# The causal mask of forgetting attention: from a bf16 product to an addition to the row of gate sums, row tiles in reverse order

## The reference

```python
log_f = jax.nn.log_sigmoid(f_logit.astype(jnp.float32) + f_bias.astype(jnp.float32))
cum = jnp.cumsum(log_f, axis=1)
...
s = jnp.einsum('bqhd,bkhd->bhqk', qb, k, preferred_element_type=jnp.float32) * scale
s = s + cb[..., None] - cum_k[:, :, None, :]
...
s = jnp.where((k_pos[None, :] <= q_pos[:, None])[None, None], s, NEG_INF)
p = jax.nn.softmax(s, axis=-1)
return jnp.einsum('bhqk,bkhd->bqhd', p.astype(v.dtype), v)
```

## Time and profile before

| What | Value |
|---|---|
| median of 3 runs | 2323.47 us |
| lowest and highest | 2323.45 and 2328.69 us |
| time of the profiled execution | 2331.4 us |
| its span, first to last instruction | 2329.6 us |
| TensorE matmul busy (PE) | 2255.2 us, 97% of the span |
| TensorE weight loads (PEld) | 1839.1 us, 79% |
| VectorE (DVE) | 1198.5 us, 51% |
| ScalarE (ACT) | 854.2 us, 37% |
| GpSimd (POOL) | 567.6 us, 24% |
| mean granted TensorE clock | 0.988 |
| the bf16 mask products, L1825, 128 of them | 29.4 us busy, 230 ns each |

### The profile page before, as it was taken

How to read it: one execution, slowest core, us unless ns; L and a number is a source line. 1 busy time by engine, 2 the same in 40 slices (tenths; PEclk the granted TensorE clock), 3 DMA queues, 4 the chain that set the end, 5 groups by cost and what they waited for, 6 DMA issues and landing times.

```text
span 2329.6 us, 32539 instructions
## 1 busy us (share of the span) xinstructions
PE 2255.2 (97%) x11512; PEld 1839.1 (79%) x11512; DVE 1198.5 (51%) x1885; ACT 854.2 (37%) x1526; POOL 567.6 (24%) x423
## 2 busy tenths in 40 slices
PE   7998898999999999999999999999899999999998
PEld 6876686888888788877888777778688888878887
DVE  5659568444444434337332476646844444443432
ACT  3127334333333312222221477733433333331223
POOL 2423332222232000110000366643222222200011
PEclk9999998999999999999999999999999999999999
DMA  7340441322221613223442877544122222162312
GB/s 230 98 105 2 154 154 33 96 87 82 81 81 63 246 56 131 90 74 117 145 153 99 219 178 179 138 153 146 37 90 87 87 88 81 63 230 72 131 48 79
DMA packets 253241, 261.20 MB, mean 112 GB/s; under 512 B 15968, under 2 KB 221024, under 8 KB 248176
## 3 DMA queue, kind: packets, MB, share of 16 engines
q1 hardware_dynamic: 242160, 220.32, 31.8%
q10 hardware_dynamic: 11008, 39.92, 4.4%
HBM read 187.92 MB, written 65.08 MB: 109 GB/s over the span
## 4 chain that ended last, share of the span: by engine, by line
PE 89%; DVE 6%; DMA 2%; ACT 1%; POOL 1%; issue 1%; SPq 0%; ACTq 0%; DVEq 0%
PE psum L1713 12%; PE psum L1714 12%; PE psum L1715 12%; PE psum L1983 11%; PE psum L1985 11%; PE psum L1987 11%; PE psum L1861 3%; PE psum L1886 3%; PE psum L1961 2%; PE psum L1963 2%; PE psum L1962 2%; PE psum L1821 1%; PE psum L1822 1%; DVE b_full L1453 1%; DVE set_lo L1472 1%; DVE b_lo L1438 1%
## 5 line engine op out<-in xcount | busy, mean ns | idle before, releaser
L1983 PE MATMUL psum<-b_hi,a_hi 128*128 128x512 f32 x1232 | 484.6, 393 | 20.6 <-DVE b_lo L1438 20.6
L1987 PE MATMUL psum<-b_hi,a_lo 128*128 128x512 f32 x1232 | 482.7, 392 | 0.0
L1985 PE MATMUL psum<-b_lo,a_hi 128*128 128x512 f32 x1232 | 482.6, 392 | 0.0
L1983 PEld LDWEIGHTS psum<-b_hi,a_hi 128*128 128x128 f32 x1232 | 233.4, 189 | 72.5 <-issue 24.1
L1713 PE MATMUL psum<-set_hi,dw_hi 128*128 128x512 f32 x704 | 274.8, 390 | 3.2 <-DVE set_lo L1472 3.2
L1714 PE MATMUL psum<-set_lo,dw_hi 128*128 128x512 f32 x704 | 273.9, 389 | 0.0
L1715 PE MATMUL psum<-set_hi,dw_lo 128*128 128x512 f32 x704 | 273.9, 389 | 0.0
L1985 PEld LDWEIGHTS psum<-b_lo,a_hi 128*128 128x128 f32 x1232 | 233.5, 190 | 48.6 <-issue 0.5
L1987 PEld LDWEIGHTS psum<-b_hi,a_lo 128*128 128x128 f32 x1232 | 233.3, 189 | 49.0
L782 POOL TENSOR_TENSOR a_sum<-a_raw 128x512 f32<-128x512 f32 x88 | 114.6, 1302 | 501.2 <-DVE a_lo L1433 442.7
L748 POOL TENSOR_TENSOR score<-score,inv_l 128x128 f32<-128x128 f32 (+7 forms) x128 | 144.9, 1147 | 355.6 <-DVE inv_l L1319 353.9
(11 more groups left out here) (205 smaller groups left out, 3604.0 us busy)
## 6 DMA issues: line engine op xcount, KB each, us to landing
a_raw<-in_ffn_w_gate_up SPq DMA_DIRECT2D x88, 512.0 KB, 5.1
hid_scr<-hid_out SPq DMA_DIRECT2D x44, 512.0 KB, 5.7
set_full<-hid_scr SPq DMA_DIRECT2D x22, 1024.0 KB, 6.2
x_t<-x_scr SPq DMA_DIRECT2D x16, 1024.0 KB, 8.3
dw_raw<-in_ffn_w_down SPq DMA_DIRECT2D x32, 512.0 KB, 3.8
x_scr<-x_t ACTq DMA_DIRECT2D x24, 512.0 KB, 2.6
w_raw<-in_fox_w_in SPq DMA_DIRECT2D x22, 512.0 KB, 4.0
w_raw<-in_swa_w_out SPq DMA_DIRECT2D x16, 512.0 KB, 4.1
```

What stands on the lines that cost most here:

```text
L1983: T.matmul(out_ps, a_hi[i][:, j, :], b_hi[i][:, j, :], start=not more and j == 0, stop=False, skip_group_check=True)
L1985: T.matmul(out_ps, a_hi[i][:, j, :], b_lo[i][:, j, :], start=False, stop=False, skip_group_check=True)
L1987: last = T.matmul(out_ps, a_lo[i][:, j, :], b_hi[i][:, j, :], start=False, stop=j == KH - 1, skip_group_check=True)
```

## The change

The list of steps is turned round: (7), (6), (5), (4), (2, 3), (0, 1). `group` now counts the tile pairs in the order in which they come, and `place` says where a result belongs; the buffers of `fox_p` swap addresses with it. The matmul L1825 is gone. Instead VectorE adds `causal_bf` to the 128 columns of `cum_all` that lie on the tile's diagonal, in place, ahead of the tile's pass. As the tiles come from last to first, a column that has been masked is no longer read by the later ones, which are narrower. The pass waits for the addition by a semaphore, `cum_turn`; in a double step the second addition also waits for the first pass. The residual `x_t` is now loaded with two of its parts after the last PV but one.

```diff
-        fox_p = [[at(f"fox_p{e}{g}", (6 * e, 12 + 8 * e)[g], [P, (6, TT)[g], 2 * P]) for g in range(2)] for e in range(2)]
+        fox_p = [[at(f"fox_p{e}{g}", (16 + 6 * e, 8 * e)[g], [P, (6, TT)[g], 2 * P]) for g in range(2)] for e in range(2)]
...
-                self.tiles = [(0, 1), (2, 3), (4,), (5,), (6,), (7,)] if self.fox else [(t,) for t in range(TT)]
+                self.tiles = [(7,), (6,), (5,), (4,), (2, 3), (0, 1)] if self.fox else [(t,) for t in range(TT)]
...
-                self.blocks = [[[(0, 0, 1), (1, 0, 2)]], [[(2, 0, 3)], [(3, 0, 4)]]] + \
-                    [[[(t, 0, 4)], [(t, 4, t - 3)]] for t in range(4, TT)] if self.fox else [[0]] * TT
+                self.blocks = [[[(t, 0, 4)], [(t, 4, t - 3)]] for t in range(TT - 1, 3, -1)] + \
+                    [[[(2, 0, 3)], [(3, 0, 4)]], [[(0, 0, 1), (1, 0, 2)]]] if self.fox else [[0]] * TT
...
+            def turns_of(self, s):
+
+                return 2 * len(self.tiles[s]) - 1
+
+            def cum_turn(self, u, e, s):
+
+                turns = [self.turns_of(i) for i in range(self.steps)]
+                return 2 * sum(turns) * u + 2 * sum(turns[:s]) + e * turns[s]
+
...
-                    if a.fox and t0 == 2:
+                    if a.fox and t0 == 4:
                         sp.wait_ge(a.pv_done, a.total)
...
-                dve.wait_ge(a.qk_done, n + 1)
                 if a.fox:
                     if s == 0:
 
                         dve.wait_ge(cum_in[e], 16 * u + 16)
-                    apart(dve)
-                    for i, t in enumerate(a.tiles[s]):
+                    else:
+
+                        wait(dve, a.max_done, n - 1)
+                    cum, turn = fox_cum(u, e), a.cum_turn(u, e, s)
+                    for i, t in reversed(list(enumerate(a.tiles[s]))):
                         here = slice(fox_at(t), fox_at(t) + fox_w(t))
-                        last = V.tensor_tensor_reduce(out=score[sl][:, here], in0=ps[:, here],
-                                                      in1=fox_cum(u, e)[:, 0:fox_w(t)],
+                        V.tensor_tensor(cols(cum, t * P), cols(cum, t * P), causal_bf[:, :], ALU.add).then_inc(cum_turn, 1)
+                        dve.wait_ge(a.qk_done, n + 1)
+                        dve.wait_ge(cum_turn, turn + a.turns_of(s) - 2 * i)
+                        apart(dve)
+                        last = V.tensor_tensor_reduce(out=score[sl][:, here], in0=ps[:, here], in1=cum[:, 0:fox_w(t)],
                                                       scale=SCALE, scalar=3.0e38, op0=ALU.add, op1=ALU.min,
                                                       accum_out=neg_max[sl][:, i:i + 1])
+                        if i:
+                            last.then_inc(cum_turn, 1)
+
+                            dve.wait_ge(cum_turn, turn + a.turns_of(s) - 1)
                     last.then_inc(a.max_done, 1)
                     return
...
-                            diagonal = cc + ww == w
                             T.matmul(ps, q_hi[:, qs], key[:, cc:cc + ww], start=True, stop=False)
-                            last = T.matmul(ps, q_lo[:, qs], key[:, cc:cc + ww], start=False,
-                                            stop=not diagonal)
-                            if diagonal:
-                                last = T.matmul(ps[:, ww - P:ww], ident_bf[:, :], causal_bf[:, :], start=False,
-                                                stop=True)
+                            last = T.matmul(ps, q_lo[:, qs], key[:, cc:cc + ww], start=False, stop=True)
```

More of the change, by code:

```diff
@@ L397, in group, with place @@
             def group(self, s):
+                return self.groups - 1 - self.place(s) if self.fox else s
+            def place(self, s):
                 return self.tiles[s][-1] // 2 if self.fox else s
+            def turns_of(self, s):
[3 more added lines that the diff above has]
+                return 2 * sum(turns) * u + 2 * sum(turns[:s]) + e * turns[s]
             def completes(self, s):
-                return not self.fox or self.tiles[s][-1] % 2 == 1
+                return not self.fox or self.tiles[s][0] % 2 == 0
         SWA_EARLY = 2
@@ L410, in trunk @@
         swa_row = sem("swa_row")
+        cum_turn = sem("fox_cum_turn")
         keys_in = [sem(f"keys_in{i}") for i in range(2)]
@@ L453, in fox_copied @@
             if f > fox.local(e, s):
-                return fox.p_dve, 2 * (fox.steps - 1) * u + 2 * (s - 1) + e + 1
+                return fox.p_dve, 2 * (fox.steps - 1) * u + 2 * s + e + 1
             return fox.p_act, 2 * fox.steps * u + 2 * s + e + 1
@@ L932, in probs_high @@
                 g = a.group(s)
-                par = g % 2
+                par = a.place(s) % 2
                 if not a.fox and s % 2:
@@ L952, in result_high @@
                 if a.fox:
+                    k = a.place(s)
                     apart(act)
-                    nc.scalar.activation(o_hi[g // 2][:, bass.ds(u, 1), g % 2 * 2 * P:(g % 2 + 1) * 2 * P],
+                    nc.scalar.activation(o_hi[k // 2][:, bass.ds(u, 1), k % 2 * 2 * P:(k % 2 + 1) * 2 * P],
                                          bank[O_BANK][:, 0:2 * P].unsqueeze(1), ACT.Copy).then_inc(a.oh_done, 1)
@@ L1330, in probs_copy @@
                 g = a.group(s)
-                if a.fox and s:
+                if a.fox and a.fills[s] > 1:
                     wait(dve, a.pv_done, a.groups * u + g - 1)
                     dve.wait_ge(a.t_done, a.fill(u, e, s) + 2)
-                    for dst, src in fox_pieces(a.blocks[s][1], a.bank_of(e, s, 1)[0], fox_p[e][g % 2]):
+                    for dst, src in fox_pieces(a.blocks[s][1], a.bank_of(e, s, 1)[0], fox_p[e][a.place(s) % 2]):
                         last = V.tensor_copy(dst, src)
@@ L1345, in result_low @@
                 if a.fox:
-                    at0 = (slice(None), bass.ds(u, 1), slice(g % 2 * 2 * P, (g % 2 + 1) * 2 * P))
-                    V.tensor_tensor(o_lo[g // 2][at0], bank[O_BANK][:, 0:2 * P].unsqueeze(1), o_hi[g // 2][at0].bitcast(FP32),
+                    k = a.place(s)
+                    at0 = (slice(None), bass.ds(u, 1), slice(k % 2 * 2 * P, (k % 2 + 1) * 2 * P))
+                    V.tensor_tensor(o_lo[k // 2][at0], bank[O_BANK][:, 0:2 * P].unsqueeze(1), o_hi[k // 2][at0].bitcast(FP32),
                                     ALU.subtract).then_inc(a.o_free, 1)
@@ L1866, in pv @@
                 g = a.group(s)
-                par, t = g % 2, a.tiles[s][-1]
+                par, t = a.place(s) % 2, 2 * a.place(s) + 1
                 pb = bank[O_BANK]
@@ L1877, in pv @@
                     pe.wait_ge(v_crossed[u // 2], 32)
-                if g == 0 and a.fox:
+                if s == 1 and a.fox:
                     pe.wait_ge(a.v_in[b], 8 * (u - b + 2))
```

1 line of the change is left out of this document (added).

## The result

The changed kernel takes 2397.0 us (median of four runs, 2391.24 to 2400.43); the kernel before, run beside it, took 2326.08 (2323.45 to 2331.74). The ratio is 1.0299, 95% interval 1.0267 to 1.0331: 3% slower. The side was forecast, the size was not: 2332.0 with a range up to 2347.

A forecast was written before the change was run, and what follows sets the result against it. TensorE's stream was taken as the bound. Stage work 220.8 us plus 22.5 idle gave 243.3 against 232.3 (+11.0), the end -2.4, together +8.6: 2332.0 us on the median, range about 2319 to 2347.

The forecast's parts named there:

- Part 1: TensorE's saturated stream: dropping 128 mask products of 0.0625 us saves 8.0 us; bounds 5 and 20.
- Part 2: VectorE: 128 additions hold it 0.32 us each (bounds 0.2, 0.45), 5.1 us a pair, raising 18.8 to 23.9.
- The self-wait: VectorE, pass waiting for its own addition's semaphore: adds 0.03 us to the addition's 0.29.
- this sum: Whole kernel: stage +11.0 us and end -2.4, together +8.6 us.
- Part 3: Reversed order: TensorE waits 1.85 us for step 8's norm in each of 8 pairs, 14.8; bounds 1.2 and 2.3.
- Part 4: Reload of the gate sums delays TensorE another 0.5 us in 7 pairs, 3.5 us; bounds 0 and 1.0 each.
- Part 5: Stage's start and end: 4.2 us TensorE idle at the start; earlier x_t load gives -2.4 at the end.
- The clock rival: TensorE's granted clock falls after repeated waits, 1.7 us each, eight of them 14: 2346 us; chance 0.08.
- The other slow rival, the reload: VectorE's run from reload to tile 5's norm stretches, 1.3 us a pair, 9 in all: 2341 us; chance 0.16.
- The first: Fast rival: additions and order are hidden, TensorE loses nothing after the fill: 2315 us; chance 0.13.
- The second: Fast rival, half the stall: TensorE waits 0.9 us a pair, no second wait: 2321 us; chance 0.18.

The follow-up runs named there:

- the kernel without a mask: Kernel before without the bf16 mask product and nothing in its place: 2323.40 us against 2330.69, ratio 0.9970.
- The PSUM variant: Changed kernel with the mask added to the scores in PSUM instead of to the gate sums in SBUF: 2350.37 us, ratio 1.0086 to the kernel before.
- order-only kernel: Changed kernel with its reversed order, but the mask product back on TensorE and no VectorE additions: 2335.4 us, ratio 1.0023 to the kernel before.
- The kernel with two SBUF operands in before's order: Kernel before, mask product kept, plus 128 unused VectorE additions of 128 columns, both operands in SBUF: 2393.36 us, ratio 1.0267.
- the variants without the contention: Changed kernel with mask added in PSUM (2350.37 us), GpSimd's norm cut to 128 columns (2340.32), or most additions issued before the reciprocal (2352.84).

## Why the prediction was right on the side and wrong on the size

**Part 1 held.** 8.0 us forecast, 7.0 measured in the kernel without a mask.

**Part 2 is the step that failed.** It priced an addition at 0.32 us with a bound of 0.45, by the slope of wider passes. Those passes have one operand in PSUM; none of the rows it went by was an SBUF-to-SBUF operation beside a norm, and it never asked which engine runs beside the addition. This is its group between 1350 and 1550 (busy us, mean ns, idle before):

```profile
L1312 DVE TENSOR_TENSOR cum_all<-cum_all,causal_bf 128x128 f32<-128x128 f32 x91 | 76.0, 835 | 4.5 <-DMA cum_all<-cum_scr 3.7
```

At 0.83 us in the mean, and with the 0.15 from its end to the start of the pass (1422.86 to 1423.01), it is 16 x (0.83 + 0.15 - 0.32) = 10.6 us a pair more than costed. A pair came out 7.3 longer than the forecast 28.3 (35.6 in the mean), so at least 3 us of that were slack. That GpSimd starts later because VectorE is held closes the ring: VectorE waits out GpSimd's instruction, GpSimd waits for VectorE's reciprocal, and VectorE shows 86% busy, GpSimd 50%.

A smaller error lies in the same step. The self-wait was priced at 0.03 us, by the chain in the earlier trace rows. In the rows above, an addition of 0.28 lets the pass start 0.43 us after its own start when the pass waits for its semaphore (1401.84 to 1402.27), and 0.20 after it when the next operation doesn't (1411.87 to 1412.07). The difference is 0.23 us, though the second of the two rows is a reciprocal and not a pass. Of a chain of copies the Trainium skill ("VectorE: DVE Perf Modes", section "The DRAIN you can't avoid") states that a semaphore after each cost nothing extra. These rows disagree where the next operation waits for that semaphore.

The contention isn't all that was missing. The PSUM variant's additions take 0.29 us, and it still costs 20 us where this sum had 8.6. How that rest divides wasn't measured.

**Part 3 held in place; its size was nearer to the low bound.** The stall was forecast at 1.85 us with the additions and 1.2 without them. The order alone shows 1.0 to 1.1. With additions of 0.29 us in PSUM it is 1.33. In the changed kernel the wait at that place is 1.38, and eight more of 0.18 to 1.17 us stand in the same pair, which the prediction didn't have.

**Part 4 was not the bound.** The reload is still waited for (4.5 us in 7 waits in the changed kernel), but the whole pair had become longer, so it had more time. In the order-only kernel it is 6.9 in 7 waits, and the pair is 28.3 with them. Its share in the 1.3 us a pair wasn't measured apart.

**Part 5.** The first 34.6 us have 7.4 us of TensorE idle time instead of 2.1, more than the 4.2 forecast, for the reason of part 2; in the order-only kernel it is 2.6. The end gave back 0.7 us in the changed kernel and 2.2 in the order-only one, of 2.4. The first QK product starts at 1306.41 instead of 1311.92, which isn't the change's doing as far as the runs tell: it is at 1312.17 and 1314.90 in two of its variants.

**The pair as a sum.** 36.30 long, 6.03 of it TensorE idle, 8% at the missing clock 2.9, together 8.9. The remaining 27.4 is 1.4 over the 26.0 of work that was forecast. Part of it may be that a wait breaks the overlap of the matmuls: seven transposes ahead of a wait hold TensorE for 0.98 us (1422.85), eight ahead of none for 0.85, start to start (1420.52 to 1421.37). The rest isn't assigned.

**The rivals.** The clock rival was given 0.08 and came in beside a larger cause. The missing clock is 6% of the stage, some 18 us of TensorE's time; what part of it the stage became longer by wasn't measured apart. The kernel with two SBUF operands in before's order loses nearly as much almost without it, and there its pairs at a clock of 0.95 are 0.35 and 0.56 us longer than those at 1.00. The other slow rival, the reload, didn't decide. The fast ones didn't come either. The first had no stall, and the order-only run has one of 1.0 to 1.1 us in each pair. The second, 0.9 us a pair and 2321, came near that stall, but the variants without the contention took 2340 to 2353 us.

**The range.** Its ends don't quite follow from the bounds given. With work -10, stalls of 1.2 and 0, start 4 and end -2.4 the low one is 2321 and not 2319, and the -10 isn't one of Part 1's bounds. The high one is 2345 and not 2347. The result lies outside either way.

## What to carry to other kernels

Before work is moved to VectorE, look where its operands lie and what GpSimd does beside it: the additions here whose tensors were all in SBUF lasted until GpSimd's running instruction was over, and those with an operand in PSUM didn't. A price taken from another row holds only for the same memories and the same neighbours, not for the column count alone. And a wait stands right before the instruction that needs it: moving one past two additions that didn't need it gave 8 us.

## What the runs showed of the hardware that was not expected

- VectorE's 128-column operation from SBUF to SBUF takes 0.27 to 0.29 us alone, and beside a GpSimd multiplication it ends 0.15 us after that one (up to 1.81 us). With one operand in PSUM it took 0.27 to 0.30 in all 128 cases of each kernel that has it.
- A `tensor_scalar` with a single SBUF operand is held up as well (0.21 alone, up to 1.68), and ends 0.09 us after GpSimd.
- The granted clock fell to 0.50 after a stretch in which TensorE was busy for 1.44 of 3 us, and came back only after some 7 us, the last 5 of them without a pause. In another variant it stayed at 1.00 after a like stretch (1.53 of 3), and fell to 0.50 three pairs later after one with the same 1.53.
- Behind a 128-column addition of 0.28 us the next operation starts 0.43 us after its start when it waits for the addition's semaphore, and 0.20 when it doesn't.
